# Two transformer blocks on one core: feed-forward nets in four groups of hidden tiles, the down projections between the block products

## The chip, the core and the metric

The kernel runs on one core of one Trainium2 chip. The metric is the device time of one execution in microseconds (us), as the median of several runs. The same core holds TensorE (PE, matrix products into PSUM), VectorE (DVE), ScalarE (ACT), GpSimd (POOL) and SyncE (SP, which only starts transfers here). All engines run their own program and meet by semaphores.

## What is computed

A sequence of 512 rows of width 1024 goes through two layers of a first block and one layer of a second. All is in float32. A layer of the first block is a feed-forward net, a mixing step (attention over a window of 128, beside a short convolution), and a second feed-forward net:

```
def swiglu(h, w_gate, w_up, w_down):
    return (jax.nn.silu(h @ w_gate) * (h @ w_up)) @ w_down

for l in range(DEPTH):                                   # DEPTH = 2
    x = x + 0.5 * swiglu(rms_norm(x, ffn1_norm[l]), ffn1_wg[l], ffn1_wu[l], ffn1_wd[l])
...
    x = x + 0.5 * swiglu(rms_norm(x, ffn2_norm[l]), ffn2_wg[l], ffn2_wu[l], ffn2_wd[l])
```

Between the two nets of a layer stands the mixing step. `w_gate` and `w_up` are 1024 x 2816, `w_down` is 2816 x 1024. So the hidden width is 22 tiles of 128 (FC = 22), the model width 8 tiles (KC = 8), and there are four such nets. The second block (a long convolution, latent attention, cross attention, a feed-forward net without a gate) is not touched.

## The kernel before

**Products.** Activations are held transposed: `x` is eight tiles of 128 x 512. A float32 product is made of rounded parts: each operand is split in a high part (`whi`, `xhi`, `hhi`, written by ACT as a copy to the type that TensorE reads) and a low rest (`wlo`, `xlo`, `hlo`, written by DVE as the difference), and each 128 x 128 x 512 tile product is three matmuls: high by high, high by low, low by high (`unit`, L695 to L697). Weights come in units of up to 8 tiles into a ring of four slots `raw`; SP starts a load when the slot's last splitting is counted in `s_split` (L533), ACT makes `whi`, DVE makes `wlo`.

**A hidden tile in the plain way** costs two units of 24 matmuls with 512 columns: its gate and its up. DVE scales both by the norm's factor, ACT takes silu, DVE multiplies, ACT and DVE make `hhi` and `hlo` of the hidden tile. `pair` does two tiles so.

**A hidden tile by Strassen's method** (`fast_pair`, L788 on) takes gate and up of one tile together as a 2 x 2 block product with seven products instead of eight. A product is `terms` (L770): 4 contraction tiles, 3 matmuls each, 256 columns. So the seven are 84 matmuls with 256 columns. Four of them use sums of weight quarters, which DVE makes in `weight_sums` (L2022 to L2027) in `tw`, and sums of input quarters `xsh` and `xsl`. Three collect in `bank_a`, from which ACT copies twice into `part[0]` and once into `part[1]` (`k_sn`), and DVE adds these to the other products (L2131, L2146, L2156; `k_ev`). The same work unit also has one plain tile: its gate is taken in two halves of 12 matmuls and its up likewise (L774 on `psS`), and these four side halves lie between the seven products, so that TensorE has work while ACT and DVE empty the banks. In order: two products, side half, two products, side half, product, side half, two products, side half. The last product (weights `dwh`, `dwl`) waits until DVE has emptied `bank_c` at L2146. In the same window DVE and ACT split the weights of the next one.

**A net before** is 11 pairs: three plain, eight with one tile by Strassen and one plain. It is made in two passes (`PASSES`): pairs 0 to 4, then the down projection of these 10 tiles (8 outputs, 30 matmuls each), then pairs 5 to 10 and the down projection of 12 tiles (36 matmuls each). A down projection alternates between two banks (`down_b`), so output m needs that DVE has added output m - 2 to `x` (L2179). In the second pass ACT and DVE also make `xhi` (L1397) and `xlo` (L2001) of each finished tile of `x`, and POOL adds its square to `acc` (L2809 to L2814), from which the next norm is taken by `norm_sum` (L740).

**What follows a net** is the mixing step, the next layer's first net, or the second block. Each begins with units that read all eight tiles of `xhi` and `xlo`, and a `norm_sum` after the first units.

## Time and profile before

| | before |
|---|---|
| median of 3 runs | 2558.33 us (2557.21 to 2558.39) |
| the profiled execution, device time | 2557.32 us |
| its span on the core | 2555.5 us |
| TensorE busy | 2535.7 us, 99% |
| DVE, ACT, POOL busy | 66%, 42%, 15% |
| read from memory | 241.84 MB, 96 GB/s over the span |

The profile names an instruction by its line in the kernel. The busy time of TensorE is taken from matmuls that overlap: one lasts 392 ns from its start to its end and the next starts 227 ns after it. So a stretch is costed by the distance of starts, not by the mean duration. "Idle before" and the engine that ended it show a wait.

### The profile page before, as it was taken

Reading aid. Unit: us, or ns where it says so; the run is one execution under the profiler, and the core shown is the slowest. Engines: PE = TensorE matmul, PEld = TensorE weight load, DVE = VectorE, ACT = ScalarE, POOL = GpSimd, SP = SyncE. Lnnn points to the kernel's source line nnn. Section 1 sums busy time; section 2 is a strip of 40 time slices with the busy share of each in tenths; the row PEclk is TensorE's granted clock in tenths of the full one; section 3 lists DMA queues with packets and bytes.
Section 4 is the critical chain, followed back from the end, with each engine's and each line's share of the span. In section 5 each row is a group of like instructions: output and inputs, shape, how many; then the busy total and the mean of one; then the engine's idle time right before and its main releaser. Section 6 shows DMA issues by size and latency. Waiting matters only on the chain.

```text
span 2555.5 us, 31807 instructions
## 1 busy us (share of the span) xinstructions
PE 2535.7 (99%) x12762; PEld 2153.3 (84%) x12762; DVE 1675.9 (66%) x2167; ACT 1062.2 (42%) x1619; POOL 381.2 (15%) x310
## 2 busy tenths in 40 slices
PE   8999999999999999999999999999999999999999
PEld 7889888888898888898888888988888888788887
DVE  8747567776476575575777755756999787642433
ACT  5434334444243343343453433433577544431332
POOL 4000021320000300001123000003186221100001
PEclk9999999999999999999999999999999999999999
DMA  5333332233333332432423323334323333233332
GB/s 153 89 118 99 87 96 85 81 99 89 96 109 90 112 90 83 124 100 83 108 66 91 100 77 107 104 93 129 90 71 80 123 92 107 83 107 95 95 99 83
DMA packets 488410, 248.12 MB, mean 97 GB/s; under 512 B 40385, under 2 KB 485062, under 8 KB 488006
## 3 DMA queue, kind: packets, MB, share of 16 engines
q1 hardware_dynamic: 487810, 245.76, 33.3%
q8 instruction: 102, 1.67, 0.3%
q10 hardware_dynamic: 452, 0.32, 0.1%
q14 instruction: 46, 0.38, 0.0%
HBM read 241.84 MB, written 4.19 MB: 96 GB/s over the span
## 4 chain that ended last, share of the span: by engine, by line
PE 95%; DVE 3%; ACT 1%; issue 0%; DMA 0%; POOL 0%; DVEq 0%
PE psT L695 10%; PE psT L697 10%; PE psT L696 10%; PE bank L695 8%; PE bank L697 8%; PE bank L696 8%; PE psS L774 5%; PE psS L775 5%; PE psS L776 5%; PE bank L776 4%; PE bank L775 4%; PE bank L774 4%; PE psS L695 1%; PE psS L697 1%; PE psS L696 1%; PE psT L776 1%
## 5 line engine op out<-in xcount | busy, mean ns | idle before, releaser
L1969 DVE TENSOR_TENSOR wlo<-raw,whi 128x1024 fp32r<-128x1024 f32 x370 | 472.1, 1277 | 320.8 <-ACT whi L1388 318.6
L1388 ACT ACTIVATE whi<-raw 128x1024 fp32r<-128x1024 f32 (+2 forms) x367 | 351.7, 960 | 392.4 <-PE psT L697 310.9
L695 PE MATMUL bank<-xhi,whi 128*128 128x512 f32 x888 | 349.4, 393 | 1.4 <-issue 1.4
L696 PE MATMUL bank<-xlo,whi 128*128 128x512 f32 x888 | 345.9, 390 | 0.0
L697 PE MATMUL bank<-xhi,wlo 128*128 128x512 f32 x888 | 345.8, 389 | 0.0
L695 PE MATMUL psT<-hhi,whi 128*128 128x512 f32 x704 | 273.9, 389 | 0.0
L696 PE MATMUL psT<-hlo,whi 128*128 128x512 f32 x704 | 273.9, 389 | 0.0
L697 PE MATMUL psT<-hhi,wlo 128*128 128x512 f32 x704 | 273.9, 389 | 0.0
L2809 POOL TENSOR_TENSOR acc<-x 128x512 f32<-128x512 f32 x8 | 8.8, 1095 | 1485.0 <-DVE x L2179 1140.2
L774 PE MATMUL psS<-xhi,whi 128*128 128x512 f32 x512 | 200.8, 392 | 0.0
L775 PE MATMUL psS<-xlo,whi 128*128 128x512 f32 x512 | 200.8, 392 | 0.0
L776 PE MATMUL psS<-xhi,wlo 128*128 128x512 f32 x512 | 199.2, 389 | 0.0
L695 PEld LDWEIGHTS bank<-xhi,whi 128*128 128x128 f32 x888 | 166.7, 188 | 36.7 <-issue 2.9
L696 PEld LDWEIGHTS bank<-xlo,whi 128*128 128x128 f32 x888 | 166.8, 188 | 35.1 <-issue 1.4
L697 PEld LDWEIGHTS bank<-xhi,wlo 128*128 128x128 f32 x888 | 166.7, 188 | 35.2
L697 PEld LDWEIGHTS psT<-hhi,wlo 128*128 128x128 f32 x704 | 132.1, 188 | 27.5
L695 PEld LDWEIGHTS psT<-hhi,whi 128*128 128x128 f32 x704 | 132.1, 188 | 27.4
L696 PEld LDWEIGHTS psT<-hlo,whi 128*128 128x128 f32 x704 | 132.1, 188 | 27.4
L1420 ACT ACTIVATE whi<-tw 128x1024 fp32r<-128x1024 f32 x64 | 67.9, 1060 | 161.1 <-PE bank L776 115.7
L2032 DVE TENSOR_TENSOR wlo<-tw,whi 128x1024 fp32r<-128x1024 f32 x64 | 78.5, 1226 | 59.0 <-ACT whi L1420 59.0
L776 PEld LDWEIGHTS psS<-xhi,wlo 128*128 128x128 f32 x512 | 96.2, 188 | 21.0
L774 PEld LDWEIGHTS psS<-xhi,whi 128*128 128x128 f32 x512 | 96.7, 189 | 16.7
(586 smaller groups left out, 5629.7 us busy)
## 6 DMA issues: line engine op xcount, KB each, us to landing
raw<-in_ffn_wg SPq DMA_DIRECT2D x88, 512.0 KB
raw<-in_ffn_wu SPq DMA_DIRECT2D x88, 512.0 KB
raw<-in_ffn_wd SPq DMA_DIRECT2D x64, 512.0 KB
raw<-in_w_mlp SPq DMA_DIRECT2D x64, 512.0 KB
raw<-in_w_in SPq DMA_DIRECT2D x53, 512.0 KB
raw<-in_ffn_wd SPq DMA_DIRECT2D x32, 256.0 KB
raw<-in_w_in SPq DMA_DIRECT2D x24, 256.0 KB
raw<-in_w_out SPq DMA_DIRECT2D x11, 512.0 KB
```

Source lines behind the costliest of these rows:

```text
L695: pe.matmul(dest, a, rhs_hi(k), start=start and k == 0, stop=False)
L696: pe.matmul(dest, a, rhs_lo(k), start=False, stop=False)
L697: mm = pe.matmul(dest, b_, rhs_hi(k), start=False, stop=stop and k == tiles - 1)
L774: pe.matmul(dest, a, mh, start=start and k == 0, stop=False, skip_group_check=resumed)
L775: pe.matmul(dest, a, ml, start=False, stop=False, skip_group_check=resumed)
L776: mm = pe.matmul(dest, b_, mh, start=False, stop=stop and k == 3, skip_group_check=resumed)
L1388: act.activation(whi[:, a:a + n], raw[:, a:a + n], ACT.Copy).then_inc(s_hi, 1)
L1420: act.activation(whi[:, 2 * i * UNIT:(2 * i + 1) * UNIT], tw[:, i * UNIT:(i + 1) * UNIT], ACT.Copy).then_inc(s_hi, 1)
L1969: dve.tensor_tensor(wlo[:, a:a + n], raw[:, a:a + n], whi[:, a:a + n].bitcast(F32), ALU.subtract).then_inc(s_split, 1)
L2032: dve.tensor_tensor(wlo[:, a:a + UNIT], tw[:, i * UNIT:(i + 1) * UNIT], whi[:, a:a + UNIT].bitcast(F32), ALU.subtract).then_inc(k_lo, 1)
L2809: pool.tensor_tensor(acc[:, :], xm, xm, ALU.mult).then_inc(s_sq, 1)
```

## The change

Each net is now a list of 17 windows of four weight units, and a closing part. Windows 0 to 2 are the plain pairs as before. Fourteen windows are `fast_window`: one tile by Strassen's method, and in the four side halves either one plain tile ("mixed", windows 3 and 14) or two outputs of the down projection of a finished group ("down", twelve windows). The groups are tiles 0 to 5, 6 to 11, 12 to 15 and 16 to 21. Windows 4 to 7 hold the eight outputs of the first group (a side half is 9 matmuls), windows 8 to 11 those of the second (9 matmuls), windows 12, 13, 15 and 16 those of the third (6 matmuls). The outputs of the last group close the net, 18 matmuls each, two banks in turn (`last_down`). The first two take tiles 16 to 20 first and tile 21, the newest, after both. So 14 of 22 tiles go by Strassen's method, where 8 did, and the down projection has the same 528 matmuls.

DVE adds an output to `x` from `psS` in its window (`side_add`). In the closing part ACT squares the finished tile of `x` and DVE adds the square to `acc`, which POOL did. POOL keeps the squares after the mixing step.

Diff, cut to its core (- before, + after):

```
-    PASSES = ((0, 5), (5, FC // 2))
-    HT = 2 * max(p1 - p0 for p0, p1 in PASSES)
+    HT = 12
+
+    WINDOWS = [("plain", 0, None), ("plain", 2, None), ("plain", 4, None)]
+    GROUPS = [(0, 6), (6, 12), (12, 16), (16, FC)]
+    WINDOWS += [("mixed", 6, None)] + [("down", 8 + i, (0, 2 * i)) for i in range(KC // 2)]
+    WINDOWS += [("down", 12 + i, (1, 2 * i)) for i in range(KC // 2)]
+    WINDOWS += [("down", 16, (2, 0)), ("down", 17, (2, 2)), ("mixed", 18, None), ("down", 20, (2, 4)), ("down", 21, (2, 6))]
+    assert WINDOWS[-1][1] == FC - 1
...
+        LAST_AT = 4 * len(WINDOWS)
+        U_FFN = LAST_AT + KC
+        FAST = len(WINDOWS) - PLAIN
+        ADDS = (len(GROUPS) - 1) * KC
+        tiles_in = lambda grp: GROUPS[grp][1] - GROUPS[grp][0]
...
+                def side_half(w, i, half, dest):
+                    kind, tile, side = WINDOWS[w]
+                    n = 4 if kind == "mixed" else tiles_in(side[0]) // 2
+                    for k in range(half * n, (half + 1) * n):
+                        a = (2 * i + 1) * UNIT + k * P
+                        if kind == "mixed":
+                            mh, ml = chunk(xhi, k), chunk(xlo, k)
+                        else:
+                            at_h = (GROUPS[side[0]][0] + k) % HT
+                            mh, ml = chunk(hhi, at_h), chunk(hlo, at_h)
+                        pe.matmul(dest, whi[:, a:a + P], mh, start=k == 0, stop=False)
+                        pe.matmul(dest, whi[:, a:a + P], ml, start=False, stop=False)
+                        mm = pe.matmul(dest, wlo[:, a:a + P], mh, start=False, stop=k == 2 * n - 1)
+                    return mm
+
+                def hidden_made(w, half):
+                    kind, tile, side = WINDOWS[w]
+                    if kind == "down" and side[1] == 0:
+                        f0, f1 = GROUPS[side[0]]
+                        pe.wait_ge(s_hl, fb + (f1 if half else (f0 + f1) // 2))
+
+                def side_free(w, i):
+                    kind, tile, side = WINDOWS[w - 1]
+                    if kind == "down":
+                        pe.wait_ge(k_xa, nf * ADDS + side[0] * KC + side[1] + 1 + i)
+                    elif i:
+                        pe.wait_ge(s_us, fb + tile + 2)
+                    else:
+                        pe.wait_ge(s_gs, fb + tile + (2 if kind == "plain" else 1))
...
                     pe.wait_ge(k_lo, 4 * g + 3)
-                    pe.wait_ge(s_gs, f if j == PLAIN else f - 1)
-                    terms(g_b, whi, wlo, UNIT, whole(0), True, False)
+                    side_free(w, 0)
+                    hidden_made(w, 0)
+                    side_half(w, 0, 0, side_b[0])
...
+                def last_down(m, k0, k1):
+                    n, f0 = tiles_in(-1), GROUPS[-1][0]
+                    for k in range(k0, k1):
+                        pe.matmul(down_b[m % 2], wcols(whi, c0 + LAST_AT + m, k), chunk(hhi, (f0 + k) % HT), start=k == 0, stop=False)
+                        pe.matmul(down_b[m % 2], wcols(whi, c0 + LAST_AT + m, k), chunk(hlo, (f0 + k) % HT), start=False, stop=False)
+                        mm = pe.matmul(down_b[m % 2], wcols(wlo, c0 + LAST_AT + m, k), chunk(hhi, (f0 + k) % HT), start=False, stop=k == n - 1)
+                    if k1 == n:
+                        mm.then_inc(s_used, 1)
+
+                for w, (kind, tile, side) in enumerate(WINDOWS):
+                    if kind == "plain":
+                        pair(q0 + 4 * w, fb + tile, w == 0)
+                    else:
+                        fast_window(w)
+                n = tiles_in(-1)
+                pe.wait_ge(k_ev, 4 * (nf + 1) * FAST - 3)
+                for k0, k1 in ((0, n - 1), (n - 1, n)):
+                    pe.wait_ge(s_hl, fb + FC - n + k1)
+                    for m in range(2):
+                        pe.wait_ge(s_split, q0 + (c0 + LAST_AT + m + 1 + RING))
+                        last_down(m, k0, k1)
+                for m in range(2, KC):
+                    pe.wait_ge(s_x, (N + 1) * KC + m - 1)
+                    pe.wait_ge(s_split, q0 + (c0 + LAST_AT + m + 1 + RING))
+                    last_down(m, 0, n)
...
+                for m in range(KC):
+                    ahead(LAST_AT + m + AHEAD)
+                    x_hi(N + 1, m)
+                    if m == 0:
+                        act.activation(acc[:, :], chunk(x, m), ACT.Square).then_inc(s_sq, 1)
+                        continue
+                    if m > 2:
+                        act.wait_ge(s_sq, (N + 1) * KC + m - 1)
+                    act.activation(tmp[m % 2][:, :], chunk(x, m), ACT.Square).then_inc(s_sqm, 1)
...
+                def side_add(w, i):
+                    m = WINDOWS[w][2][1] + i
+                    dve.wait_ge(s_used, q0 + c0 + 4 * w + 2 + 2 * i)
+                    dve.scalar_tensor_tensor(chunk(x, m), psS[:, i * S:(i + 1) * S], 0.5, chunk(x, m), ALU.mult,
+                                             ALU.add).then_inc(k_xa, 1)
...
+                    if before == "mixed":
+                        plain_up(w - 1)
+                    elif before == "down":
+                        side_add(w - 1, 1)
+                    whole_lo(w, 1)
+                    if before == "mixed":
+                        hidden_lo(w - 1, False)
...
+                    if mixed:
+                        dve.wait_ge(s_used, c + 2)
+                        dve.tensor_tensor(tmp[0][:, :], psS[:, 0:S], inv[:, :], ALU.mult).then_inc(s_gs, 1)
+                    else:
+                        side_add(w, 0)
...
+                side_add(len(WINDOWS) - 1, 1)
+                for m in range(KC):
+                    ahead(LAST_AT + m + AHEAD)
+                    dve.wait_ge(s_used, q0 + c0 + LAST_AT + m + 1)
+                    dve.scalar_tensor_tensor(chunk(x, m), down_b[m % 2], 0.5, chunk(x, m), ALU.mult, ALU.add).then_inc(s_x, 1)
+                    x_lo(N + 1, m)
+                    if m:
+                        dve.wait_ge(s_sqm, N * (KC - 1) + m)
+                        dve.wait_ge(s_sq, (N + 1) * KC + m)
+                        dve.tensor_tensor(acc[:, :], acc[:, :], tmp[m % 2][:, :], ALU.add).then_inc(s_sq, 1)
...
-                squares(l * 3 + 1)
                 mix(l)
                 squares(l * 3 + 2)
-                squares(l * 3 + 3)
+            pool.wait_ge(s_x, (FINAL1 + 1) * KC)
```

DVE around the start of a window, before: from the last steps of one window of a pair to the first of the next. `tmp_86` is the Strassen tile's up and hidden tile, `tmp_85` the plain tile's.

```order
232 L2158 TENSOR_TENSOR tmp_86<-tmp_86,inv 128x512
233 L2161 TENSOR_TENSOR tmp_86<-tmp_86,tmp_84 128x512
234 L2043 TENSOR_TENSOR dwl<-raw,dwh 128x512
235 L2116 TENSOR_TENSOR hlo<-tmp_86,hhi 128x512
236 L2108 TENSOR_TENSOR tmp_85<-psS,inv 128x512
237 L2111 TENSOR_TENSOR tmp_85<-tmp_85,tmp_83 128x512
238 L2038 TENSOR_TENSOR wlo<-raw,whi 128x1024
```

The same place after, between two windows of the third group (12 and 13):

```order
257 L2202 TENSOR_TENSOR tmp_86<-tmp_86,inv 128x512
258 L2205 TENSOR_TENSOR tmp_86<-tmp_86,tmp_84 128x512
259 L2078 TENSOR_TENSOR dwl<-raw,dwh 128x512
260 L2154 TENSOR_TENSOR hlo<-tmp_86,hhi 128x512
261 L2148 SCALAR_TENSOR_TENSOR x<-psS,x 128x512
262 L2073 TENSOR_TENSOR wlo<-raw,whi 128x512
263 L2172 TENSOR_TENSOR tmp_84<-psT,part_97 128x256
264 L2049 TENSOR_TENSOR cwl<-raw,cwh 128x1024
265 L2057 TENSOR_TENSOR tw<-raw 128x1024
```

The scaling and the product of the plain tile, and its rest, have gone; one addition to `x` stands there, and the rest of the side weights is half as wide.

ACT at the end of a net, before, two outputs of the down projection:

```order
185 L1388 ACTIVATE whi<-raw 128x512
186 L1388 ACTIVATE whi<-raw 128x1024
187 L1397 ACTIVATE xhi<-x,gains 128x512
188 L1388 ACTIVATE whi<-raw 128x512
189 L1388 ACTIVATE whi<-raw 128x1024
190 L1397 ACTIVATE xhi<-x,gains 128x512
```

ACT there after, outputs 0 and 1 of the closing part:

```order
222 L1422 ACTIVATE whi<-raw 128x768
223 L1431 ACTIVATE xhi<-x,gains 128x512
224 L1563 ACTIVATE acc<-x 128x512
225 L1422 ACTIVATE whi<-raw 128x768
226 L1431 ACTIVATE xhi<-x,gains 128x512
227 L1567 ACTIVATE tmp_84<-x 128x512
```

DVE there after, the same outputs and the next unit:

```order
354 L2004 TENSOR_TENSOR wlo<-raw,whi 128x768
355 L2219 SCALAR_TENSOR_TENSOR x<-psT,x 128x512
356 L2036 SCALAR_TENSOR_TENSOR xlo<-x,gains,xhi 128x512
357 L2004 TENSOR_TENSOR wlo<-raw,whi 128x768
358 L2219 SCALAR_TENSOR_TENSOR x<-psT,x 128x512
359 L2036 SCALAR_TENSOR_TENSOR xlo<-x,gains,xhi 128x512
360 L2224 TENSOR_TENSOR acc<-acc,tmp_84 128x512
361 L2004 TENSOR_TENSOR wlo<-raw,whi 128x768
```

Each output now has one unit of weights to split instead of two, and a square on ACT and an addition on DVE that stood on POOL.

## Rows read from the trace of the kernel before

**Rows 1.** The page: busy time by engine, and the granted clock in 40 slices.
```profile
PE 2535.7 (99%) x12762; PEld 2153.3 (84%) x12762; DVE 1675.9 (66%) x2167; ACT 1062.2 (42%) x1619; POOL 381.2 (15%) x310
...
PEclk9999999999999999999999999999999999999999
```

**Rows 2.** TensorE's waits: line, who ended it, us in total, times, longest.
```profile
PE psS L967 <- POOL frow L2858: 3.8, 1, 3.8
...
PE bank L774 <- issue: 1.4, 1, 1.4
```

**Rows 3.** Timeline of TensorE, one window: start us, duration us, line, output and operands.
```profile
220.28 0.28 PE L774 MATMUL bank<-xhi,cwh 128*128 128x256 f32 x1
...
223.15 0.40 PE L774 MATMUL psS<-xhi,whi 128*128 128x512 f32 x1
...
225.90 0.28 PE L774 MATMUL bank<-xsh,whi 128*128 128x256 f32 x1
...
228.77 0.40 PE L774 MATMUL psS<-xhi,whi 128*128 128x512 f32 x1
...
241.32 0.28 PE L774 MATMUL bank<-xhi,cwh 128*128 128x256 f32 x1
```

**Rows 4.** The same window by busy time of each engine, then clock, DMA share, GB/s.
```profile
220.28:241.32 21.04, 21.04 (x133) 19.07 (x132) 15.49 (x22) 8.83 (x13) 0.00 (x0) 1.00 0.34 100
```

**Rows 5.** Timeline of DVE from that window into the next.
```profile
237.34 0.42 DVE L2148 TENSOR_TENSOR tmp<-bank,inv 128x256 f32<-128x256 f32 x1 [2.90 <-PE bank L776]
...
238.49 1.23 DVE L2032 TENSOR_TENSOR wlo<-tw,whi 128x1024 fp32r<-128x1024 f32 x1 [0.40 <-ACT whi L1420]
239.63 0.41 DVE L2156 TENSOR_TENSOR tmp<-bank,part 128x256 f32<-128x256 f32 x1
240.08 0.69 DVE L2158 TENSOR_TENSOR tmp<-tmp,inv 128x512 f32<-128x512 f32 x1
240.81 0.69 DVE L2161 TENSOR_TENSOR tmp<-tmp,tmp 128x512 f32<-128x512 f32 x1
241.42 0.68 DVE L2043 TENSOR_TENSOR dwl<-raw,dwh 128x512 fp32r<-128x512 f32 x1
...
246.21 1.21 DVE L2014 TENSOR_TENSOR cwl<-raw,cwh 128x1024 fp32r<-128x1024 f32 x1
247.34 1.22 DVE L2022 TENSOR_TENSOR tw<-raw 128x1024 f32<-128x1024 f32 x1
248.59 0.69 DVE L2025 TENSOR_TENSOR tw<-tw,raw 128x512 f32<-128x512 f32 x1
249.31 0.69 DVE L2027 TENSOR_TENSOR tw<-raw,tw 128x512 f32<-128x512 f32 x1
```

**Rows 6.** Timeline of ACT, two of its steps beside these.
```profile
237.39 1.06 ACT L1420 ACTIVATE whi<-tw 128x1024 fp32r<-128x1024 f32 x1 [3.76 <-PE bank L776]
...
241.53 0.63 ACT L1483 ACTIVATE hhi<-tmp 128x512 fp32r<-128x512 f32 x1 [2.04 <-DVE tmp L2161]
```

**Rows 7.** Start of one 512 KB load on SP's queue.
```profile
229.00 0.39 SPq L533 DMA_DIRECT2D raw<-in_ffn_wg  x1
```

**Rows 8.** Stretches after that start, columns as in rows 4.
```profile
230.00:232.70 2.70, 2.70 (x18) 2.43 (x17) 1.92 (x2) 1.01 (x2) 0.00 (x0) 1.00 0.67 194
232.70:236.00 3.30, 3.30 (x19) 2.81 (x18) 1.56 (x2) 0.93 (x3) 0.00 (x0) 1.00 0.00 0
```

**Rows 9.** Timeline at the end of a net, down projection of 12 tiles.
```profile
345.44 0.69 DVE L2179 SCALAR_TENSOR_TENSOR x<-psT,x 128x512 f32<-128x512 f32 x1 [0.34 <-PE psT L697]
346.17 0.72 ACT L1397 ACTIVATE xhi<-x,gains 128x512 fp32r<-128x512 f32 x1 [2.33 <-DVE x L2179]
346.92 0.87 DVE L2001 SCALAR_TENSOR_TENSOR xlo<-x,gains,xhi 128x512 fp32r<-128x512 f32 x1 [0.79 <-ACT xhi L1397]
347.72 1.77 DVE L1969 TENSOR_TENSOR wlo<-raw,whi 128x512 fp32r<-128x512 f32 x1
...
369.92 0.69 DVE L2179 SCALAR_TENSOR_TENSOR x<-psT,x 128x512 f32<-128x512 f32 x1 [0.34 <-PE psT L697]
```

**Rows 10.** Timeline of TensorE: the next norm's sum.
```profile
375.17 0.59 PE L740 MATMUL psO<-acc,ones 128*128 128x512 f32 x1
```

**Rows 11.** Timeline of TensorE, the one wait for an addition to `x`, in cross attention.
```profile
2074.29 0.39 PE L697 MATMUL psT<-xhi,wlo 128*128 128x512 f32 x1
2074.94 0.50 PE L695 MATMUL psT<-xhi,whi 128*128 128x512 f32 x1 [0.26 <-DVE x L2638]
```

More of the change, by code:

```diff
@@ L471, in build, with side_cols @@
                 bank_of[("hq", s // 2 + 1)], bank_of[("hk", s // 2 + 1)] = bank[0][:, :], bank[1][:, :]
-        assert U_LAYER % RING == 0 and all(u % RING == 0 for u in PAIR_AT) and U_FFN % RING == 0 and U_MIX % RING == 0
-        FAST_AT = {PAIR_AT[j]: j for j in (PLAIN, PASSES[1][0])}
-        UNIT_TILES = {DOWN_AT[ps] + 2 * m + j: down_tiles(ps, j) for ps in range(2) for m in range(KC) for j in range(2)}
+        assert U_LAYER % RING == 0 and U_FFN % RING == 0 and U_MIX % RING == 0
+        UNIT_TILES = {LAST_AT + m: tiles_in(-1) for m in range(KC)}
         QUARTERS_AT = {1: 0, 2: 1, 3: 2, 2 * PLAIN - 1: 3}
         EARLY = 2 * PLAIN - 2
+        def side_cols(w):
+            kind, tile, side = WINDOWS[w]
+            return UNIT if kind == "mixed" else tiles_in(side[0]) * P
         def slot(c):
@@ new lines, in hidden_made @@
+                def hidden_made(w, half):
+                    kind, tile, side = WINDOWS[w]
+                    if kind == "down" and side[1] == 0:
[3 more added lines that the diff above has]
+                    kind, tile, side = WINDOWS[w - 1]
+                    if kind == "down":
+                        pe.wait_ge(k_xa, nf * ADDS + side[0] * KC + side[1] + 1 + i)
[3 more added lines that the diff above has]
+                        pe.wait_ge(s_gs, fb + tile + (2 if kind == "plain" else 1))
@@ L829, in fast_pair @@
                     terms(bank_c, dwh, dwl, 0, summed(3), False, True, True).then_inc(k_pe, 1)
-                    terms(u_b, whi, wlo, 3 * UNIT + S, whole(4), False, True).then_inc(s_used, 1)
-                def down(ps):
-                    for m in range(KC):
-                        if m < 2:
-                            if ps:
-                                pe.wait_ge(k_xa, nf * KC + KC - 1 + m)
-                        elif ps:
-                            pe.wait_ge(s_x, (N + 1) * KC + m - 1)
-                        else:
-                            pe.wait_ge(k_xa, nf * KC + m - 1)
-                        if m == 0:
-                            pe.wait_ge(k_ev, 4 * (nf * FAST + PASSES[ps][1] - PLAIN) - 3)
-                        for j in range(2):
-                            tiles = down_tiles(ps, j)
-                            if m == 0:
-                                pe.wait_ge(s_hl, fb + 2 * PASSES[ps][0] + 8 * j + tiles)
-                            unit(c0 + DOWN_AT[ps] + 2 * m + j, q0, down_b[m % 2], tiles,
-                                 lambda k, j=j: chunk(hhi, 8 * j + k), lambda k, j=j: chunk(hlo, 8 * j + k),
-                                 start=j == 0, stop=j == 1)
@@ new lines, in ffn @@
+                for w, (kind, tile, side) in enumerate(WINDOWS):
+                    if kind == "plain":
[9 more added lines that the diff above has]
+                        last_down(m, k0, k1)
```

247 lines of the change are left out of this document (100 added, 147 removed).

## Prediction

> **What bounds the kernel now.** I read the page first. TensorE is busy for 2535.7 of 2555.5 us at the full clock (2.4 GHz) in nearly every slice [rows 1]. Its list of waits is short: 3.8 us at the very start, one wait of 1.4 us in the first net, and some smaller ones [rows 2]. So the time is the number of matmuls times their distance. DVE (66%) and ACT (42%) cost nothing while they keep up [rows 1]. The reader is to see two things: that an edit is worth what it takes from TensorE's stream, and that it can lose this again only where DVE or ACT comes late.
>
> Then I read one window of the kernel before in order of time [rows 3], which gives the two prices. From 223.15 to 225.90 lie 12 matmuls with 512 columns: 2.75 us. Over many in a row one takes 0.2267 us: a down projection output of 36 takes 8.16 us, since L2179 stands at 345.44 and at 369.92, three outputs on [rows 9]. From 225.90 to 228.77 lie 24 with 256 columns: 2.87 us, 0.1196 each. So half the columns is a little over half the price. The window starts at 220.28 and the next at 241.32, which is 21.04 us [rows 3]. It holds 84 narrow and 48 wide matmuls: 84 x 0.1196 = 10.04 and four side halves of 2.75 = 11.00, sum 21.04. The stream has no gap.
>
> **The products.** A plain tile costs 48 wide matmuls, 48 x 0.2267 = 10.88 us. A Strassen tile costs 21.04 - 10.88 = 10.16 us (the small price of changing width is in it). The difference is 0.72 us. The change turns 6 more tiles of each of four nets: 24 x 0.72 = 17.3 us off TensorE, and all of TensorE is on the path. The down projections keep their 528 matmuls a net. They only move, so they cost nothing by themselves.
>
> Against the whole net: before, eight windows of 21.04 and 22 x 24 wide matmuls (119.7) are 288.0 us. After, two mixed windows (42.1), eight with side halves of 9 (10.04 + 4 x 2.07 = 18.32 each, 146.6), four with side halves of 6 (10.04 + 4 x 1.39 = 15.60, 62.4) and the closing 8 x 18 wide ones (32.6) are 283.7 us. The difference is 4.3 us a net, 17.3 in all.
>
> The rows show these distances directly. The Trainium skill (TensorE: Matmul & The Clock Gate, section Back-to-back issue gap) gives N / 2.4 + 2.5 ns for a warm matmul of N columns. By it a tile would save 48 x 0.2158 - 84 x 0.1092 = 1.19 us and the change 28.5 us. The trace disagrees on both widths, and more on the narrow one (119.6 against 109.2 ns), so the sum does not use it.
>
> **DVE and ACT in the shorter windows.** This decides whether the 17.3 us arrive. In a window of 21.04 us DVE is busy for 15.49 us and ACT for 8.83 [rows 4]. A down window drops four DVE steps of 512 columns (scale of gate and up, the product, the rest of the hidden tile) and adds two additions. From one start to the next a step of 1024 columns takes 1.14 us, one of 512 takes 0.61, or 0.73 where it needs the one before, one of 256 takes 0.34 to 0.45 [rows 5]. So DVE saves 0.61 + 0.72 + 0.61 + 0.61 = 2.55 and adds 1.22. Its two rests of side weights shrink from 1.14 each to 0.61 (group of 4 tiles) or about 0.87 (6 tiles, between the two). That leaves 15.49 - 2.55 + 1.22 - 1.06 = 13.1 us of 15.60, and 13.6 of 18.32. DVE fits, and ACT easily.
>
> A sum that fits can still stall by its order, so I walked the narrowest window, T being its start on TensorE. The sixth of the seven products of the window before ends at T - 2.82 (1.43 for the seventh and 1.39 for the last side half). DVE reads it 0.21 later (the step at 237.34 [rows 5] after the product that ended at 237.13, by the distances above). ACT rounds the last weight sums (1.06 [rows 6]), and DVE stands at L2032 at T - 1.46. Then, with the distances of rows 5: L2156 at T - 0.32, L2158 at T + 0.13, L2161 at T + 0.86, L2043 at T + 1.47. ACT makes `hhi` at T + 1.58 (0.72 after L2161 [rows 5, 6]), `hlo` follows at T + 2.24, the addition at 2.85, the rest of the side weights at 3.46, L2131 at 4.07, L2014 at 4.40, and L2022 could start at 5.53. Here is the one place where a **load** comes near. L2022 reads a unit whose load SP can start only after L2043, at T + 2.2. A lone load that started at 229.00 moved its data until about 232.7 and none later [rows 7, 8], so it lands about 3.7 us on, at T + 5.9. DVE waits some 0.4 us, as it doesn't before. Then L2025 at 7.2, L2027 at 8.0, ACT's rounding, L2032 at 9.1, the addition at 10.2, the rest at 10.8, L2146 at 11.4 to 11.85. TensorE needs this last one for the seventh product, which starts at 10.04 x 6/7 + 3 x 1.39 = T + 12.8. Slack is 0.9 us, and 0.4 in the one window per net whose successor is mixed (a rest of 1024 columns). All other waits of the window have over 0.7 us. After L2146 DVE waits over 1 us for TensorE, so lateness doesn't add up. I take no stall in the 48 down windows. The bounds are 0 and, where the load lands 1 us later than the row's, 0.1 to 0.6 in each of the 16 narrow ones.
>
> **The closing part.** Let E be the end of the last window. Tile 21 is ready by about E + 2.4 (L2161 at E + 0.9 as above, `hhi`, `hlo`), and TensorE wants it after 30 wide matmuls, at E + 6.8: no wait. But output 0 now ends at E + 7.48 and output 1 at 8.16, only 0.68 us apart where it was 8.16. Output 2 needs the bank of output 0. DVE starts its addition about 0.2 after the end and takes 0.69 [rows 9], so TensorE may go on at E + 8.41: 0.25 late, and the first matmul after such a wait costs about 0.1 more (0.34 to the next start, seen behind the one wait of this kind [rows 11]). That is a **new wait** of 0.38 us, with bounds 0.25 (no price for going on) and 0.65 (DVE a quarter of a microsecond later than the row). Four nets: 1.5 us.
>
> From there an output takes TensorE 4.08 us. DVE's cycle is addition to `xhi` 0.73, to `xlo` 0.75, to the next 0.80 [rows 9], the square's addition 0.61, the split of 768 columns 0.87: 3.76 us, and about 4.05 for the last three, whose split is of 1024. It fits. The same split took 1.77 us for 512 columns beside POOL's square [rows 9]; POOL is idle here now, so I use the undisturbed 0.61 scaled. DVE begins this part late, though (addition 1 at E + 11.3, when TensorE ended output 1 at 8.16), and catches up only 0.3 us per output. Its last addition starts about 1.9 us after TensorE's end, where before it started 0.2 after [rows 9].
>
> What follows was built with slack. In the mixing step the sum of squares is wanted at 375.17, 24 matmuls after the end at 369.73, so 5.44 us on [rows 10]. The squares will be ready 1.88 + 0.73 + 0.75 + 0.80 + 0.69 = 4.85 after the end. `xlo` of tile 7 has about 0.5 us left. Where a net is followed by another net or by the second block the slack is thinner; I put 0 to 1.7 (the whole lateness) on each of the four ends and take 0.2, since the one end that I can work out has 0.5 to spare. That is 0.7 us in all.
>
> **Sum.** The profiled execution took 2557.32 us, span 2555.5 and 1.8 around it. 2557.3 - 17.3 + 1.5 + 0.7 = 2542.2. The median of the runs is 1.0 above the profiled one: 2543.2, I say **2543**, a gain of 0.6%. Start and end of the program, the plain pairs, and window 3 with the 1.4 us wait before it stand as they were.
>
> **Rivals.**
> - *All hidden.* The additions and the ends cost nothing: 2558.3 - 17.3 = 2541.0. For it: every wait here is under 0.5 us. Against: the wait at output 2 is plain arithmetic. Chance 0.12.
> - *The closing part becomes DVE's.* If DVE's cycle there is 4.5 us and not 3.8 (its first three steps include two hand-overs to ACT), outputs 3 to 7 each lose 0.4, and the next stage about 1 more: 3 us a net, 12 in all, 2555. It decides from a cycle of 4.1. Half of that gives 2549. Chance 0.09.
> - *Slower: the down windows become DVE's and ACT's.* The place is the wait of the seventh product for L2146, in all 48 windows. If the loads and hand-overs (some eight in a window) cost so much more that the loop takes 16.3 in the narrow and 19.0 in the wide windows, each loses 0.7 us: 34 us, 2543 + 34 = 2577. For it: DVE is at 84% of a narrow window, and the loads have come within a few tenths of being late. Against: the wide windows have 2.7 us more to spare than the narrow ones. It takes a mean stall of 0.32 to lose the gain, and 0.42 to be slower by 0.2%. With the narrow windows alone at 0.7 the time is 2554. Chance 0.13, half of it for the mild form.
> - *The narrow matmuls cost half of the wide ones.* Then a tile saves 10.88 - 84 x 0.1134 = 1.36 us and the time is about 2528. The page's figure named above leads the same way, to 2532. Rows 3 speak against both. Chance 0.01.
>
> **How the numbers follow.** The forecast has 0.65. Its own range is 2541 to 2546, from the bounds of the new wait (1.0 to 2.6) and of the ends (0 to 3). To hold 8 in 10 the range takes in the case of all hidden and the half-strength form of the second rival: 2540 to 2551. A measurement of this kernel tells about 0.2% (5 us) from no change, that is, below 2553.2 is faster and above 2563.4 slower. Faster: 0.65 + 0.12 + 0.01, 0.05 of the second rival and 0.02 of the third, 0.85. Same: the other 0.04 of the second and 0.05 of the third's mild form, 0.09. Slower: 0.06.
>
> **What would show it.** TensorE's starts 18.3 us apart in windows 4 to 11 and 15.6 apart in 12, 13, 15 and 16, and 12762 + 864 = 13626 matmuls. DVE waiting a few tenths for a load at the line of L2022 in the narrow windows, and TensorE waiting for no DVE line there. One wait of some 0.3 us per net for the addition to `x` in the closing part. The last addition of a net 1.9 us after TensorE's end. If TensorE waits for the line of L2146, or the starts in the narrow windows are over 16 apart, the third rival holds. If there is a wait at each closing output, the second does. It would also be wrong if the distance of narrow matmuls beside the hidden tiles is not that beside `xhi`.

## The result and the profile after

The changed kernel takes 2541.75 us (median of 4 runs, 2541.55 to 2542.86), the kernel before 2558.28 in the runs beside it. The ratio is 0.9938, with a 95% interval of 0.9923 to 0.9953: 0.6% faster, 16.5 us. The forecast was 2543.

The profiled execution of after took 2541.64 us, its span is 2539.8 (before: 2557.32 and 2555.5). The page, with the columns of [rows 1]:

```profile
PE 2519.7 (99%) x13626; PEld 2177.9 (86%) x13626; DVE 1834.5 (72%) x2475; ACT 1143.8 (45%) x1771; POOL 303.9 (12%) x250
...
PEclk9999999999999999999999999999999999999999
```

There are 864 matmuls more and TensorE is busy for 16.0 us less, at the same clock. DVE has 159 us more work and GpSimd 77 less, the squares at the ends of the nets. Against [rows 2], TensorE's list of waits has no new line:

```profile
PE psS L1001 <- POOL frow L2900: 3.8, 1, 3.8
...
PE bank L783 <- issue: 1.4, 1, 1.4
...
PE psT L704 <- DVE x L2680: 0.3, 1, 0.3
```

Timeline of TensorE at the start of three windows, the last wide one's end among them (columns as in [rows 3]; L783 is L774 of before):

```profile
249.06 0.28 PE L783 MATMUL bank<-xhi,cwh 128*128 128x256 f32 x1
...
264.66 0.28 PE L783 MATMUL bank<-xhi,cwh 128*128 128x256 f32 x1
...
280.26 0.28 PE L783 MATMUL bank<-xhi,cwh 128*128 128x256 f32 x1
```

These narrow windows are 15.60 us apart. The wide ones are 18.32 apart (230.74 to 249.06), the mixed ones 21.04, in each of the four nets; only the very first mixed one takes 22.72, with the 1.4 us wait of [rows 2] in it. The same by busy time, columns as in [rows 4]: two narrow windows, the second followed by a mixed one, and a wide one.

```profile
249.06:264.66 15.60, 15.60 (x110) 14.57 (x108) 12.48 (x19) 7.06 (x11) 0.00 (x0) 1.00 0.36 102
264.66:280.26 15.60, 15.60 (x110) 14.57 (x108) 13.57 (x20) 7.38 (x11) 0.00 (x0) 1.00 0.46 135
157.46:175.78 18.32, 18.32 (x122) 16.82 (x120) 13.84 (x20) 7.49 (x11) 0.00 (x0) 1.00 0.34 101
```

TensorE's 15.60 and 18.32 us are full. The tightest place is in the second of these, on DVE (L2057, L2190 and L2192 are L2022, L2146 and L2148 of before):

```profile
270.54 1.23 DVE L2057 TENSOR_TENSOR tw<-raw 128x1024 f32<-128x1024 f32 x1 [0.28 <-DMA raw<-in_ffn_wu]
...
274.76 0.68 DVE L2148 SCALAR_TENSOR_TENSOR x<-psS,x 128x512 f32<-128x512 f32 x1
275.36 1.22 DVE L2073 TENSOR_TENSOR wlo<-raw,whi 128x1024 fp32r<-128x1024 f32 x1
276.49 0.42 DVE L2190 TENSOR_TENSOR tmp<-bank,part 128x256 f32<-128x256 f32 x1
277.63 0.42 DVE L2192 TENSOR_TENSOR tmp<-bank,inv 128x256 f32<-128x256 f32 x1 [0.72 <-PE bank L785]
```

L2190 ends at 276.91. The seventh product starts at 277.43 (the six products before it and three side halves put it 12.77 into the window): slack 0.52 (0.57 to 0.61 in the other nets). In the other narrow windows it is 1.0 to 1.7, in the wide ones 2.4.

The one new wait is at closing output 2, too short for the list of waits. TensorE, with the distances 0.49 and 0.34 where 0.227 is usual:

```profile
340.43 0.39 PE L872 MATMUL psT<-hhi,wlo 128*128 128x512 f32 x1
340.92 0.50 PE L870 MATMUL psT<-hhi,whi 128*128 128x512 f32 x1
341.26 0.39 PE L871 MATMUL psT<-hlo,whi 128*128 128x512 f32 x1
```

That is 0.26 + 0.11, and it stands in the same form in the other nets (the first of the three rows at 857.01, 1207.31 and 1723.93). DVE's closing cycle (L2219 is the addition to `x`), and its last addition:

```profile
347.41 0.68 DVE L2219 SCALAR_TENSOR_TENSOR x<-psT,x 128x512 f32<-128x512 f32 x1
348.88 0.75 DVE L2036 SCALAR_TENSOR_TENSOR xlo<-x,gains,xhi 128x512 fp32r<-128x512 f32 x1 [0.79 <-ACT xhi L1431]
349.55 0.69 DVE L2224 TENSOR_TENSOR acc<-acc,tmp 128x512 f32<-128x512 f32 x1
350.15 0.95 DVE L2004 TENSOR_TENSOR wlo<-raw,whi 128x768 fp32r<-128x768 f32 x1
351.02 0.69 DVE L2219 SCALAR_TENSOR_TENSOR x<-psT,x 128x512 f32<-128x512 f32 x1
...
366.92 0.68 DVE L2219 SCALAR_TENSOR_TENSOR x<-psT,x 128x512 f32<-128x512 f32 x1
```

The cycle is 3.61 us, 4.09 for the last three. The down projection's last matmul ends by its distance at 365.54, so the last addition is 1.38 us late. In [rows 9] this was 0.2. Nothing waits for it.

### The profile page after: what moved, and what is told of

Same layout as the page of the kernel before. It is cut to its first block, busy times and chain, and to the rows that moved or that the text cites. A ratio compares the mean times of both kernels' runs of the same rounds, so it can differ in the third digit from the quotient of the medians.

```text
span 2539.8 us, 34207 instructions
## 1 busy us (share of the span) xinstructions
PE 2519.7 (99%) x13626; PEld 2177.9 (86%) x13626; DVE 1834.5 (72%) x2475; ACT 1143.8 (45%) x1771; POOL 303.9 (12%) x250
## 4 chain that ended last, share of the span: by engine, by line
PE 95%; DVE 3%; ACT 1%; issue 0%; DMA 0%; POOL 0%; DVEq 0%; ACTq 0%
PE bank L704 8%; PE bank L706 8%; PE bank L705 8%; PE bank L785 6%; PE bank L784 6%; PE bank L783 6%; PE psS L804 6%; PE psS L805 6%; PE psS L806 6%; PE psT L704 4%; PE psT L705 4%; PE psT L706 4%; PE psT L870 2%; PE psT L872 2%; PE psT L871 2%; PE psS L704 1%
## 5 line engine op out<-in xcount | busy, mean ns | idle before, releaser
L2004 DVE TENSOR_TENSOR wlo<-raw,whi 128x1024 fp32r<-128x1024 f32 (+1 forms) x274 | 362.0, 1323 | 114.8 <-ACT whi L1422 111.6
L1422 ACT ACTIVATE whi<-raw 128x1024 fp32r<-128x1024 f32 (+1 forms) x271 | 277.4, 1026 | 131.9 <-PE psT L706 92.4
L804 PE MATMUL psS<-hhi,whi 128*128 128x512 f32 x512 | 201.7, 394 | 0.0
L805 PE MATMUL psS<-hlo,whi 128*128 128x512 f32 x512 | 201.5, 394 | 0.0
L806 PE MATMUL psS<-hhi,wlo 128*128 128x512 f32 x512 | 199.2, 389 | 0.0
L783 PE MATMUL bank<-xsh,whi 128*128 128x256 f32 x672 | 189.6, 282 | 1.4 <-issue 1.4
L785 PE MATMUL bank<-xsh,wlo 128*128 128x256 f32 x672 | 190.2, 283 | 0.0
L784 PE MATMUL bank<-xsl,whi 128*128 128x256 f32 x672 | 190.1, 283 | 0.0
L783 PEld LDWEIGHTS bank<-xsh,whi 128*128 128x128 f32 x672 | 128.5, 191 | 6.3 <-issue 1.8
L784 PEld LDWEIGHTS bank<-xsl,whi 128*128 128x128 f32 x672 | 128.5, 191 | 4.3
L2192 DVE TENSOR_TENSOR tmp<-bank,inv 128x256 f32<-128x256 f32 x56 | 23.8, 425 | 131.2 <-PE bank L785 131.2
```

Of the source, the lines that this page charges most:

```text
L783: pe.matmul(dest, a, mh, start=start and k == 0, stop=False, skip_group_check=resumed)
L784: pe.matmul(dest, a, ml, start=False, stop=False, skip_group_check=resumed)
L785: mm = pe.matmul(dest, b_, mh, start=False, stop=stop and k == 3, skip_group_check=resumed)
L804: pe.matmul(dest, whi[:, a:a + P], mh, start=k == 0, stop=False)
L805: pe.matmul(dest, whi[:, a:a + P], ml, start=False, stop=False)
L806: mm = pe.matmul(dest, wlo[:, a:a + P], mh, start=False, stop=k == 2 * n - 1)
```

## Experiments

All spans are of profiled executions and stand against 2539.8 (after) or 2555.5 (before). "Late" is the start of a net's last addition, counted from TensorE's end of the down projection.

### The new wait at output 2

```diff
-                for k0, k1 in ((0, n - 1), (n - 1, n)):
...
-                    for m in range(2):
+                for m, k0, k1 in ((0, 0, n - 1), (1, 0, 2), (0, n - 1, n), (1, 2, n)):
...
                         last_down(m, k0, k1)
```

> The changed kernel with one edit: in the closing part of a net the matmuls of outputs 0 and 1 go in the order (output 0, tiles 0-4), (1, 0-1), (0, 5), (1, 2-5) instead of (0, 0-4), (1, 0-4), (0, 5), (1, 5). Output 0 then ends at E + 5.4 us and output 1 at E + 8.16, E being the end of the last window. Theory (the 0.38 us at output 2 are only the addition of output 0 coming 0.25 us late, plus 0.1 for going on): the wait is gone in all four nets, no other takes its place (tile 21 is wanted at E + 4.8 and is ready at E + 2.4), and the span falls by 1.5 us, from 2539.8 to 2538.3. The addition of output 7 then starts under 0.6 us after TensorE's end instead of about 1.8. Rival: DVE's late start is set by the end of its window work or by tile 21's rest, so the wait moves to before tile 21's matmuls or to output 3, and the span stays within 0.3 us.

Measured: 2540.15 us, span 2538.4. The expected 1.5 us are there, 1.4 of them by the spans; by TensorE's starts each net gains 0.375 at output 2. Its timeline has no gap there any more, and DVE's last addition comes 0.23 after TensorE's end at 365.54:

```profile
340.15 0.39 PE L872 MATMUL psT<-hhi,wlo 128*128 128x512 f32 x1
340.38 0.39 PE L870 MATMUL psT<-hhi,whi 128*128 128x512 f32 x1
...
365.77 0.68 DVE L2218 SCALAR_TENSOR_TENSOR x<-psT,x 128x512 f32<-128x512 f32 x1
```

So the wait was the addition of output 0 and nothing behind it. With DVE only 0.23 late instead of 1.38, nothing more was won, so these 1.38 us had cost nothing.

### Who makes the squares

In the second run the changed kernel's squares go back to GpSimd. On ACT, DVE and GpSimd:

```diff
-                    act.activation(tmp[m % 2][:, :], chunk(x, m), ACT.Square).then_inc(s_sqm, 1)
...
-                        dve.tensor_tensor(acc[:, :], acc[:, :], tmp[m % 2][:, :], ALU.add).then_inc(s_sq, 1)
...
+                squares(l * 3 + 1)
                 mix(l)
                 squares(l * 3 + 2)
...
+                squares(l * 3 + 3)
```

> The changed kernel with the squares of the closing part back where they were before the change: GpSimd makes and adds them, ACT makes none and DVE adds none. DVE's own work in a closing output falls by 0.6 us. Theory (DVE runs slowly beside GpSimd's 128x512 step, as in the kernel before, where a split of 512 columns took 1.77 us there): DVE's cycle is 4.0 to 4.4 us instead of 3.62, so that with an output of 4.08 us on TensorE it does not catch up; the last addition starts 2 to 3.5 us after TensorE's end instead of about 1.8, and the span grows by 0 to 1 us per net. Rival (GpSimd's step costs DVE nothing, and moving the squares was needless): the cycle falls to 3.0 us, DVE has caught up by output 4, and the span stays within 0.3 us of 2539.8.

Measured: 2552.64 us, span 2550.6, 10.8 us slower than after. DVE and GpSimd in one closing cycle:

```profile
345.04 0.87 DVE L2030 SCALAR_TENSOR_TENSOR xlo<-x,gains,xhi 128x512 fp32r<-128x512 f32 x1 [0.79 <-ACT xhi L1431]
345.84 2.04 DVE L1998 TENSOR_TENSOR wlo<-raw,whi 128x768 fp32r<-128x768 f32 x1
347.81 0.68 DVE L2213 SCALAR_TENSOR_TENSOR x<-psT,x 128x512 f32<-128x512 f32 x1
...
344.33 1.04 POOL L2844 TENSOR_TENSOR sqt<-x 128x512 f32<-128x512 f32 x1 [2.10 <-DVE x L2213]
345.45 1.62 POOL L2846 TENSOR_TENSOR acc<-acc,sqt 128x512 f32<-128x512 f32 x1
```

The split of 768 columns takes 2.04 us instead of 0.95, the cycle is 4.24 (4.0 to 4.4 expected) and 4.50 for the last three, and the last addition is 4.0 us late, where I had expected 2 to 3.5. The mechanism was right and its price too low. I had allowed 0 to 1 us a net; by TensorE's starts the nets lose 2.2, 3.9, 2.1 and 2.1. TensorE loses nothing more at the closing outputs, it stands behind the net:

```profile
PE bank L704 <- DVE xlo L2030: 4.4, 3, 1.5
...
PE bank L713 <- ACT xhi L1431: 2.1, 1, 2.1
```

The second net loses more than the others because TensorE's clock is lower behind its stand:

```profile
890.07 0.50 PE L713 MATMUL bank<-xhi,whi 128*128 128x512 f32 x1 [2.10 <-ACT xhi L1431]
...
890.00:893.90 3.90, 3.83 (x10) 3.03 (x11) 3.03 (x2) 0.96 (x2) 1.99 (x2) 0.58 0.44 129
```

Eight matmuls are 0.427 us apart there instead of 0.227, which is 1.6 of the 10.8 us. The ten runs of this kernel have spans of 2549.2 to 2549.3, 2550.6 to 2550.9 and 2552.3. Steps of about 1.5 would fit none, one or two such stretches, but only the profiled run can show them.

To tell lateness from another effect of GpSimd's work, the same with the order of the first experiment:

> The squares of the closing part on GpSimd, as in the second experiment, and outputs 0 and 1 in the order of the first. Theory (what the second experiment lost came from one thing, DVE's last addition 4.0 us after TensorE's end, and the stage behind a net bears 1.7 to 2.3 us of it): with DVE's first addition some 2.3 us earlier, the cycles of 4.24 and 4.5 us remain, the last addition is about 2.1 us late, and only the second net's end waits (about 0.4 us) and the sum behind the others a few tenths: span 2539 to 2541, where GpSimd's squares alone gave 2550.6. Rival (GpSimd's work itself delays the stage behind the net, through its own sum or by slowing DVE there): it keeps over half of the loss, span over 2544.

Measured: 2542.68 us, span 2541.0. The last additions are 2.34 to 2.40 late, and the loss against the first experiment (2538.4) is 2.6 us, not 10.8. So most of the loss is lateness. By TensorE's starts the stage behind the second net bears 1.7 us of it in both runs (TensorE waits 0.65 here and 2.27 there), the stages behind the other three 2.35 (almost no wait here, 1.6 to 1.7 there). But the rival of the expectation has a part. Behind these three nets TensorE comes to the norm's sum some 0.2 us before GpSimd's own addition is done, and with the going on it loses 0.44 in each, in both runs. That is 1.3 of the 2.6 us here, and 1.3 of the 10.8 there. And the squares' move alone, in the kernel before (ACT's and DVE's lines of the diff above with a plus, GpSimd's with a minus):

> The kernel before with one part of the change alone: the squares at the end of a net are made by ACT and added by DVE instead of by GpSimd. Theory (the move is worth something only where a closing output is short; here an output takes 8.16 us on TensorE, and DVE's cycle fits with and without it): span 2555.5 within 0.3, DVE's split of 512 columns there down from 1.77 to 0.7 us. Rival (GpSimd's slowing of DVE also cost the kernel before something at the ends of its nets): 0.5 to 2 us faster.

Measured: 2557.47 us beside 2557.36, span 2555.5. DVE there:

```profile
346.81 0.75 DVE L2007 SCALAR_TENSOR_TENSOR xlo<-x,gains,xhi 128x512 fp32r<-128x512 f32 x1 [0.79 <-ACT xhi L1397]
347.47 0.69 DVE L2192 TENSOR_TENSOR acc<-acc,tmp 128x512 f32<-128x512 f32 x1
348.08 0.69 DVE L1975 TENSOR_TENSOR wlo<-raw,whi 128x512 fp32r<-128x512 f32 x1
```

The split went from 1.77 [rows 9] to 0.69 us, and it was worth nothing, with 8.16 us per output. The same edit is worth 10.8 us where an output takes 4.08 (1.6 of them by the clock): two thirds of the whole gain hang on it.

### How near the down windows are to DVE

One useless step ahead of L2190's wait, in the 48 down windows:

```diff
+                    if not mixed:
+                        dve.reciprocal(tmp[2][:, 0:192], inv[:, 0:192])
                     dve.wait_ge(k_pe, 5 * g + 4)
```

> The changed kernel with one useless step more on DVE in each of the 48 down windows, a reciprocal of 128x192, about 1.3 us, placed right ahead of the eviction that lets TensorE start its seventh product. Theory (that eviction is 2.4 us early in the eight wide windows of a net, and 1.4, 0.5, 1.2 and 1.7 early in the four narrow ones): only the second narrow window stalls, by 0.8 us, the third by 0.1; the whole is 3 to 5 us slower, span about 2543.5. Rival A (DVE is the bound of the down windows, each of its microseconds counts): 48 x 1.3 = 62 us. Rival B (the narrow windows only look tight, the later steps absorb it): under 0.5 us.

Measured: 2546.67 us, span 2545.1, 5.3 more. TensorE waits in the second narrow window of each net for the eviction (L2192 here), and in the third one of the last net:

```profile
276.96 1.35 DVE L2189 RECIPROCAL tmp<-inv 128x192 f32<-128x192 f32 x1
278.23 0.36 DVE L2192 TENSOR_TENSOR tmp<-bank,part 128x256 f32<-128x256 f32 x1
...
278.74 0.36 PE L783 MATMUL bank<-xsh,dwh 128*128 128x256 f32 x1 [0.78 <-DVE tmp L2192]
```

This window takes 16.60 instead of 15.60 (16.51 in one net), the third 15.77 (16.04 in the last net, where its slack was 1.0), the others what they took. 48 x 1.3 us more on DVE cost 5 us, not 62. With the reciprocal of 512 columns:

> The same with a reciprocal of 128x512, about 3.35 us. Theory: each wide window stalls 3.35 - 2.4 = 1.0 us (8 x 1.0), the narrow ones 2.0, 2.8, 2.1 and 1.6: 16 us a net, 65 in all, span about 2605. If what DVE is left with at the end of a stretched window is handed on to the next one, it is more, up to 90. Rival A (every microsecond counts): 48 x 3.35 = 161 us. Rival B: under 10 us.

Measured: 2608.73 us, span 2607.0, 67.2 more where the slacks gave 65.

```profile
PE bank L783 <- DVE tmp L2192: 50.1, 48, 2.2
```

All 48 windows wait now. The wide ones are 19.23 apart (0.91 more; the slack of 2.4 gave 1.0; the last of a net 18.85), the first narrow one 17.49 (1.89 more). The four narrow ones start their seventh product 1.8, 2.4, 2.1 and 1.6 us later than before (2.4 for the third in the last net), where the slacks gave 2.0, 2.8, 2.1 and 1.6. All these waits together are 61.5 us beside the expected 65. The other 5.8 us are TensorE's clock, which was lower for about 3 us behind four of the waits (last section). So it is in part luck that 67.2 is so near to 65. The slacks read in the timeline are right to 0.4 us all the same, and for its 0.7 us in every window the third rival of the prediction would have needed 1.2 to 3.1 us more on DVE in each.

### The price of one Strassen tile

The kernel before with one tile of a net less by Strassen's method:

```diff
-    PLAIN = 3
+    PLAIN = 4
```

> The kernel before with seven Strassen tiles in each net instead of eight (the first Strassen tile made plain). It measures the price of one conversion by itself, without down windows and without the new closing part. Theory (a conversion is worth 48 x 0.2267 - (84 x 0.1196 + small change) = 0.72 us on TensorE): the span grows by 4 x 0.72 = 2.9 us, from 2555.5 to 2558.4, and a matmul count lower by 36 x 4 = 144. Rival A (narrow matmuls cost half of the wide ones): + 4 x 1.36 = 5.4 us. Rival B (1.19 us by N / 2.4 + 2.5 ns, the Trainium skill, TensorE: Matmul & The Clock Gate, section Back-to-back issue gap): + 4.8 us.

Measured: 2558.86 us beside 2557.69, span 2557.0 and 12618 matmuls. The span grew by 1.5 us, half of the 2.9 expected. But the 1.4 us wait at L774 [rows 2] is gone from TensorE's list as well, since the window in which it stood is plain now. I had not foreseen that. The ends of the four nets on TensorE tell the two apart: 368.83, 890.06, 1244.96 and 1766.18, where they were 369.72, 890.22, 1244.40 and 1764.91. The first is 0.89 earlier, and each of the next three nets adds 0.71 to 0.73. So a tile is worth 0.72 in three nets by themselves, where the rivals gave 1.36 and 1.19, and in the first net the vanished wait gave 1.6 back. Why this wait of the first net vanishes with the window, the trace doesn't tell, since it names only "issue".

### Sixteen Strassen tiles: where the short groups go

First the short groups last, so that the closing part has four tiles:

```diff
-    GROUPS = [(0, 6), (6, 12), (12, 16), (16, FC)]
...
+    GROUPS = [(0, 6), (6, 10), (10, 14), (14, 18), (18, FC)]
...
```

> The changed kernel with sixteen Strassen tiles in each net: groups of 6, 4, 4, 4, 4 tiles, so that no mixed window is left and the last group has four tiles. On TensorE a net takes 8 wide and ... in all sixteen down windows: four of 18.32 and twelve of 15.60 us, and eight closing outputs of 24/2 = 12 matmuls, 2.72 us each, 282.3 instead of 283.7 us: 5.8 us less for four nets. But DVE's cycle in the closing part was 3.62 us with an output of 4.08. Theory (the second rival's mechanism, DVE's cycle over the output's time): outputs 2 to 7 each wait about 0.8 us, 5 us a net, and the next stage waits for the last additions as well, 1 to 2 us more: 14 to 22 us slower than the changed kernel, span 2548 to 2560. Rival (the cycle's hand-overs to ACT shrink or overlap when it is pressed): it is 0 to 6 us faster, span 2534 to 2540.

Measured: 2566.26 us, span 2564.9, 25 slower than after and worse than the 14 to 22 expected. All down windows keep 15.60 and 18.32, twelve narrow ones in a row. The loss lies behind them:

```profile
PE psT L868 <- DVE x L2217: 8.1, 16, 1.1
PE bank L702 <- DVE xlo L2034: 5.8, 3, 1.9
...
PE bank L711 <- ACT xhi L1429: 2.4, 2, 2.0
```

Outputs 4 to 6 start 3.35 us apart instead of 2.72 and output 7 starts 4.09 after output 6, the last addition is 4.6 us late, and TensorE's clock is lower for some microseconds after it stood from 372.43 to 374.75:

```profile
372.00:374.70 2.70, 0.81 (x4) 0.35 (x2) 1.91 (x4) 1.24 (x2) 0.00 (x0) 1.00 0.32 73
374.70:377.90 3.20, 3.15 (x6) 1.81 (x7) 2.04 (x5) 2.26 (x3) 0.00 (x0) 0.59 0.45 102
377.90:381.00 3.10, 3.10 (x13) 2.52 (x12) 3.10 (x4) 2.60 (x3) 0.00 (x0) 0.88 0.65 147
```

This part of the loss was not in my sum. Then with DVE's closing steps reordered, so that `xlo` and the square of output m - 1 follow addition m, and with the order of outputs 0 and 1:

```diff
-                    x_lo(N + 1, m)
-                    if m:
...
+                    for e in ((m - 1,) if m < KC - 1 else (m - 1, m)):
...
+                        x_lo(N + 1, e)
```

> The sixteen tiles again, with the order of the first experiment for outputs 0 and 1, and DVE's closing steps in another order: the addition of output m is followed by x_lo and the square's addition of output m - 1, so that DVE does not stand while ACT rounds x_hi. DVE's cycle should be 0.73 less, 0.61 + 0.75 + 0.6 + 0.87 = about 2.9 us against an output of 2.72 (3.2 for the last three). Theory: 0.2 to 0.5 us of wait at outputs 2 to 7, and 0.5 to 1 at the end: 2 to 3.5 us a net, which eats the 5.8 us of the products; span 2538 to 2548. Rival (the wait per output is hidden by the two banks and the 1.5 us of the order are won too): span 2532 to 2536.

Measured: 2557.86 us, span 2557.5; I had expected 2538 to 2548. DVE no longer stands for ACT's `xhi`, and the first cycles fell to 3.13. The last four additions are 4.09 us apart all the same:

```profile
363.79 0.72 ACT L1428 ACTIVATE xhi<-x,gains 128x512 fp32r<-128x512 f32 x1 [1.89 <-DVE x L2216]
364.42 0.61 ACT L1564 ACTIVATE tmp<-x 128x512 f32<-128x512 f32 x1
364.94 1.04 ACT L1419 ACTIVATE whi<-raw 128x1024 fp32r<-128x1024 f32 x1
...
366.01 1.23 DVE L2001 TENSOR_TENSOR wlo<-raw,whi 128x1024 fp32r<-128x1024 f32 x1 [1.00 <-ACT whi L1419]
367.15 0.68 DVE L2216 SCALAR_TENSOR_TENSOR x<-psT,x 128x512 f32<-128x512 f32 x1
```

It is a ring of two engines: addition, `xhi`, square, split on ACT, split on DVE, addition; 0.72 + 0.63 + 0.52 + 1.07 + 1.14 = 4.08. The 3.13 of the first cycles is the same ring with splits of 512 columns, and it too is over the 2.72 of an output. My 2.9 and 3.2 counted DVE's work alone. The changed kernel stands at the same 4.09 in its last three outputs, with 4.08 us of TensorE's beside it. The control, fourteen tiles with both edits:

> The changed kernel (fourteen Strassen tiles) with both edits: order of outputs 0 and 1 and the reordered DVE steps. Theory (nothing in the closing part but the wait at output 2 is on the path): the same as with the order alone, span 2538.3, 1.5 us less than the changed kernel, and DVE's reordering is worth nothing (under 0.3 us). Rival: the ends of the nets have a hidden cost, and the last addition's steps coming in another order move it by 0.3 to 1 us a net either way.

Measured: 2540.12 us, span 2538.3, as with the order alone. DVE's reordering is worth nothing there.

Last, the short groups first, and the closing part with six tiles as in the changed kernel:

```diff
-    GROUPS = [(0, 6), (6, 12), (12, 16), (16, FC)]
...
+    GROUPS = [(0, 4), (4, 8), (8, 12), (12, 16), (16, FC)]
...
```

> Sixteen Strassen tiles once more, but with the short groups first: 4, 4, 4, 4 and then 6 tiles, so that all sixteen windows are narrow down windows (15.60 us) and the closing part keeps its six tiles (4.08 us per output), as in the changed kernel; outputs 0 and 1 in the changed kernel's order. On TensorE a net is 16 x 15.60 + 32.65 = 282.3 us, the same products as the run with groups of 6, 4, 4, 4, 4. Theory (that run lost its time in the closing part alone, where DVE and ACT need 3.1 to 4.1 us per output and TensorE had 2.72): nothing stalls here but the 0.38 us at output 2, and each net is 1.44 us shorter than in the changed kernel: span 2539.8 - 5.8 = 2534.0. Rival (sixteen narrow windows in a row wear out the half microsecond by which DVE is early, or more Strassen tiles cost time wherever the groups lie): over 2540.

> The same with outputs 0 and 1 in the order of the first experiment. Theory: both gains add, 5.8 + 1.4 us: span 2532.6, time 2534.4, 0.3% faster than the changed kernel. Rival (with the wait gone, the next thing is late by as much): as the run without the order, 2534.

Measured: span 2534.3 and 2532.6 us (expected 2534.0 and 2532.6), times 2536.07 and 2534.43. All 64 windows of 16 Strassen tiles and 4 nets run 15.60 apart (but the very first, which has the 1.4 us wait of [rows 2] in it). The same products as in the first run with sixteen tiles take 30.6 us less by the place of the long group alone. The last version is faster than both kernels: 0.9908 of the kernel before (0.9892 to 0.9925), and 7.2 us of span under the changed one.

## Why the prediction was right

**The products** (17.3 us) arrived in full. Window distances of 18.32, 15.60 and 21.04 and the count of 13626 are as forecast, and the run with seven tiles gives 0.72 for a tile by itself, in three nets one by one.

**The down windows** did not stall. DVE's busy time was forecast as 13.1 in a narrow window and measured 12.48 and 13.57 in the two shown; the second has one step more between its ends, and one rest of side weights of 1024 columns instead of 512. 13.6 for a wide one measured 13.84. The slack of the tightest window was forecast as 0.4 and measured 0.52, that of the other narrow ones as 0.9 and measured 1.0 to 1.7. In the tightest window L2172 stood at T + 4.05 (forecast 4.07). The wait for a load was forecast as 0.4 in the narrow windows. It is 0.16 to 0.46 and comes fifteen times, six in narrow windows and nine in wide ones, where it has room. The two runs with a useless step confirm the slacks by time, not only by rows.

**The new wait** was forecast as 0.38 us and four times, and is 0.37. The bounds of 0.25 and 0.65 were not needed, since all its terms came from rows of the same lines.

**The closing cycle** was forecast as 3.76 and measured 3.61. The step that failed is the 0.80 from `xlo` to the next. It was read beside GpSimd's square [rows 9], like the 1.77 that I did discount; alone it is 0.67. The late last addition (1.9 forecast, 1.38 measured) follows from it.

**The ends of the nets** were priced at 0.7 us in all and cost nothing: the first experiment takes the lateness away and gains only its own wait. The bound of 0 held. The slack worked out for the mixing step (lateness of 1.88 with about 0.5 left) was right: the runs with GpSimd's squares show that this stage bears 2.35. What was put too high is the share for the ends that could not be worked out. The one behind the second net bears 1.7 and the one behind the fourth 2.35, both more than the 1.34 to 1.38 that came.

**From profile to median** I added the 1.0 us by which the kernel before's median lay above its profiled run. After's median lies 0.1 above. This term was 0.9 too high and that of the ends 0.7, together a little more than the 1.3 us between 2543 and 2541.75. Without them the sum is 2557.3 - 17.3 + 1.5 = 2541.5, and the profiled run was 2541.64.

**The rivals.** The second (closing part DVE's, deciding from a cycle of 4.1) is nearer than its 0.09 sounds, since the last three outputs stand at 4.09. Its size for 4.5 us (12 in all) is near to what GpSimd's squares cost (10.8), but its place was wrong. I had outputs 3 to 7 wait 0.4 each. None did: an output needs the addition of the output two before, so lateness of up to one output is carried, and all of it was paid behind the net, a part of it through the clock. The third rival (down windows) needed over 2.4 us more on DVE in a wide window, and 0.5 to 1.7 in a narrow one, before that window stalls.

## What to carry to other kernels

Where one engine is full, price an edit by what it takes from that engine's stream, and then read the slack of the steps beside it in microseconds at the place where they are waited for: here that gave the time within 0.05%, and stretching one step by known amounts confirmed it. When work is cut into groups, the last group is the one that nothing covers, so make it long and the covered ones short; here the same products differ by 30 us by that alone. A step taken from a row where another engine disturbed it must be discounted as a whole, with the steps beside it, and a chain that passes between two engines has to be summed as a ring, not engine by engine.

## What the runs showed of the hardware

**DVE beside GpSimd.** With GpSimd's steps from SBUF beside it, DVE's split of two SBUF operands took 2.04 us for 768 columns (0.95 alone) and 2.16 for 1024 (1.23 alone). The addition that reads PSUM and `x` kept its 0.68 us, but in these rows GpSimd was idle then. The added time follows what GpSimd's step had still to run. The splits of 768 and of 1024 columns began 1.23 and 1.08 us before its end (347.07 and 359.77) and took 1.09 and 0.93 longer than alone. Two steps `xlo` began 0.39 and 0.33 before the end of a shorter one and took 0.19 and 0.12 longer. So all four end as if they had stood until 0.14 to 0.21 us before GpSimd's recorded end. That agrees with the Trainium skill (SBUF — State Buffer, section SBUF: two separate sides), by which a VectorE step with two SBUF inputs and a GpSimd step that reads SBUF share a pair of ports as an exclusive lock, the one that comes second being blocked for the whole of the other's instruction.

**The clock.** In the kernels before and after, the granted clock is 9 tenths or more of 2.4 GHz in all 40 slices. In the run with a closing part of four tiles, after outputs with waits and a stand of 2.3 us (372.43 to 374.75), the granted clock was 0.59 in the next 3.2 us and 0.88 in the 3.1 after that: part of these at the 1.2 GHz level. In the run with GpSimd's squares it was 0.58 over 3.9 us behind the second net, after a full stream and a stand of 2.5 us (887.58 to 890.07), and stayed at 1.00 behind the first net after one of 1.9 us (370.25 to 372.17). The run with the reciprocal of 512 columns has one and the same wait in the second narrow window of each net, and what follows it is different in the first and the second net (the longer rows have the columns of [rows 4]):

```profile
289.10 0.35 PE L783 MATMUL bank<-xsh,dwh 128*128 128x256 f32 x1 [2.20 <-DVE tmp L2192]
289.10:293.10 4.00, 4.00 (x28) 3.74 (x29) 3.88 (x7) 1.66 (x3) 0.00 (x0) 1.00 0.00 0
...
822.30 0.35 PE L783 MATMUL bank<-xsh,dwh 128*128 128x256 f32 x1 [2.20 <-DVE tmp L2192]
823.30:827.30 4.00, 4.00 (x17) 3.42 (x16) 3.49 (x6) 1.83 (x4) 0.00 (x0) 0.57 0.00 0
```

So the length of the stand does not decide by itself. In the lower stretches matmuls of 512 columns start 0.427 us apart instead of 0.227, those of 256 columns 0.213 instead of 0.120. What decides was not tested.
